# A forward transform over four token residues, and two placements around it

## The reference

```python
def hyena_filters(L, ...):
    ...                                   # a small network over positions gives h [L, order, 2, width]
    kern = concat([fwd, zeros(1), bwd[:0:-1]], axis=0)
    kern = kern / sum(abs(kern), axis=0)  # the filter norms
    return rfft(kern, axis=0)

def long_conv(u, k_f, skip):              # L = 512 tokens
    y = irfft(rfft(u, n=2 * L) * k_f, n=2 * L)[:L]
    return y + u * skip

z = parts[0]
for o in range(2):                        # two orders
    z = parts[o + 1] * long_conv(z, k_f[:, o], skip[o])
return (z * silu(gate)) @ w_out
```

## Time and profile before

| what | value |
| --- | --- |
| runs | 2197.36 us median of 3 (2193.96 to 2201.46) |
| profiled execution | 2202.59 us, span 2200.8 us |
| PE busy | 2095.3 us, 95% |
| PEld busy | 1611.6 us, 73% |
| DVE busy | 1372.0 us, 62% |
| ACT busy | 816.5 us, 37% |
| POOL busy | 797.9 us, 36% |

### The profile page before, as it was taken

The page is one execution under the profiler, slowest core; times in us unless marked ns, Lnnn a source line. Parts: engine busy times, 40 slices in busy tenths (PEclk is TensorE's granted clock), DMA queues, the critical chain, the costliest instruction groups (busy, mean ns, idle before and its releaser), DMA issues. The chain is left out here.

```text
span 2200.8 us, 28268 instructions
## 1 busy us (share of the span) xinstructions
PE 2095.3 (95%) x11070; PEld 1611.6 (73%) x11070; DVE 1372.0 (62%) x2351; ACT 816.5 (37%) x1185; POOL 797.9 (36%) x478
## 2 busy tenths in 40 slices
PE   7949999999999999999999999999999989999998
PEld 6847788888878877888888866556877536777776
DVE  8563399995555567488882133358775674477752
ACT  3414333333233377333332242345663332322222
POOL 6614455554545511344444411121002432311232
PEclk9979999999999999999999999998999979999999
DMA  5032344443434511244443322021002213222311
GB/s 187 2 44 86 102 138 144 140 130 114 128 117 129 128 40 25 86 144 144 144 134 90 96 101 79 29 58 41 1 21 78 91 63 141 80 77 78 114 58 67
DMA packets 57891, 201.84 MB, mean 92 GB/s; under 512 B 10521, under 2 KB 11721, under 8 KB 54207
## 3 DMA queue, kind: packets, MB, share of 16 engines
q1 hardware_dynamic: 40464, 156.92, 22.6%
q0 software_dynamic: 13568, 41.94, 6.2%
q10 hardware_dynamic: 3728, 1.18, 0.3%
HBM read 179.04 MB, written 10.49 MB: 86 GB/s over the span
## 5 line engine op out<-in xcount | busy, mean ns | idle before, releaser
L1666 POOL TENSOR_TENSOR w_lo<-raw,w_hi 128x1024 fp32r<-128x1024 f32 (+1 forms) x224 | 564.8, 2522 | 828.3 <-ACT w_hi L1222 828.1
L1222 ACT ACTIVATE w_hi<-raw 128x1024 fp32r<-128x1024 f32 (+1 forms) x224 | 233.8, 1045 | 847.5 <-PE psum L678 654.6
L671 PE MATMUL psum<-h_hi,w_hi 128*128 128x512 f32 x800 | 319.1, 399 | 1.5 <-ACT h_hi L1316 1.0
L672 PE MATMUL psum<-h_hi,w_lo 128*128 128x512 f32 x800 | 311.7, 390 | 0.0
L678 PE MATMUL psum<-h_lo,w_hi 128*128 128x512 f32 x800 | 198.0, 389 | 0.0
L671 PE MATMUL psum<-f_lo,w_hi 128*128 128x512 f32 x480 | 189.6, 395 | 2.3 <-POOL w_lo L1666 2.2
L672 PE MATMUL psum<-f_lo,w_lo 128*128 128x512 f32 x480 | 187.2, 390 | 0.0
L671 PEld LDWEIGHTS psum<-h_hi,w_hi 128*128 128x128 f32 x800 | 150.3, 188 | 38.5 <-ACT h_hi L1316 3.3
L672 PEld LDWEIGHTS psum<-h_hi,w_lo 128*128 128x128 f32 x800 | 150.3, 188 | 32.1 <-issue 2.2
L678 PEld LDWEIGHTS psum<-h_lo,w_hi 128*128 128x128 f32 x800 | 150.0, 188 | 31.3 <-issue 0.2
L1212 ACT ACTIVATE big<-psum 128x384 f32<-128x384 f32 (+6 forms) x182 | 90.0, 532 | 164.9 <-PE psum L973 47.6
(11 more groups left out here) (433 smaller groups left out, 4167.9 us busy)
## 6 DMA issues: line engine op xcount, KB each, us to landing
raw<-in_ffn_w_up SPq DMA_DIRECT2D x88, 512.0 KB, 3.6
raw<-in_ffn_w_down SPq DMA_DIRECT2D x32, 512.0 KB, 3.6
raw<-in_hy_in SPq DMA_DIRECT2D x32, 512.0 KB, 5.7
ffn_buf<-in_ada_w POOLq DMA_DIRECT2D x28, 512.0 KB, 5.0
sq<-in_ada_w POOLq DMA_DIRECT2D x20, 512.0 KB, 5.4
raw<-in_ssm_w_glu SPq DMA_DIRECT2D x16, 512.0 KB, 3.6
spec<-big SPq DMA_DIRECT2D x8, 1024.0 KB, 4.1
big<-spec SPq DMA_DIRECT2D x8, 1024.0 KB, 4.8
```

Source lines behind the costliest of these rows:

```text
L671: pe.matmul(o, hi[:, k, :], h_of(k), start=k == 0, stop=False)
L672: pe.matmul(o, lo[:, k, :], h_of(k), start=False, stop=False)
L1222: act.activation(w_parts(n)[0], raw[:, (n % 4) * HALF:(n % 4) * HALF + w], ACT.Copy).then_inc(S["w_hi"], 1)
L1666: pool.tensor_tensor(lo, raw[:, (n % 4) * HALF:(n % 4) * HALF + w], hi.bitcast(F32), ALU.subtract) \
```

## The change

The forward transform no longer folds even and odd tokens with 256 frequencies. It takes the four residues of the token number modulo 4 and 128 frequencies, cosine and sine, one matmul call each: eight calls per pass in two steps of four (`z_quarters`). The other frequencies follow from two levels of sums on VectorE: `z_first` (eight operations of 512 columns per pass, in two steps) into `YW`, and `z_fold` (one of 1024 and two of 512 for each u) into `CS`. The products follow the fold in the same tile. `YW` is now written by `z_first` too, so `z_first` of a pass waits for the inverse of the pass before. The four tables have new tiles. The frequencies of the second half stand in reverse order, in the filters' transform too. The new table (`QUARTERS`, 512 KB) is loaded by GpSimd's queue after the filters' transforms, over a part of the old table that is then no longer read.

Besides, the filter norm stands behind the transforms of its unit on TensorE and behind the fold on VectorE, `FSUM` has two buffers, seven `keep_clock` matmuls stand before the first cumulative sums of the attention, and in the gate tiles ScalarE makes `z_hi(t - 1)` before the activation of tile t.

```diff
-        TURN_AT = {8: (0, 0), 11: (0, 1), 15: (1, 0), 19: (1, 1)}
-        SPECTRUM_AT = {9: 0, 10: 1, 12: 2, 14: 3, 16: 4, 18: 5, 20: 6, 22: 7}
-        BACK_AT = {13: (0, 0), 17: (0, 1), 21: (1, 0), 24: (1, 1)}
-        SPEC_LOAD_AT = {t + 4: u + 1 for t, u in SPECTRUM_AT.items() if u < 7} | {9: 0}
+        TURN_AT = {5: (0, 0), 9: (0, 1), 15: (1, 0), 20: (1, 1)}
+        QUARTER_AT = {6: (0, 0), 7: (0, 1), 12: (1, 0), 13: (1, 1), 18: (2, 0), 19: (2, 1), 23: (3, 0), 24: (3, 1)}
+        PRODUCT_AT = {8: 0, 9: 1, 14: 2, 15: 3, 20: 4, 21: 5, 25: 6, 26: 7}
+        BACK_AT = {11: (0, 0), 17: (0, 1), 22: (1, 0), 27: (1, 1)}
+        QUARTER_OF = (((0, 0), (0, 2), (1, 1), (1, 3)), ((0, 1), (0, 3), (1, 0), (1, 2)))
+        SPEC_LOAD_AT = {t + 4: u + 1 for t, u in PRODUCT_AT.items() if u < 7} | {6: 0}
...
@@ TensorE, cumulate
                 if h == 0:
+                    keep_clock(7, 7)
                     pe.wait_ge(S["neg_ready"], 2)
...
@@ TensorE, filter stage
                 if u < 3:
                     filters(u + 1)
-                    filter_norm(u)
                 for f in range(2):
...
                         fills(i, key)
+                if u < 3:
+                    filter_norm(u)
...
@@ TensorE, hyena stage
+            def z_quarters(p_, part):
+
+                if p_ == 0 and part == 0:
+                    pe.wait_ge(S["quarters_in"], 16)
+                for i_, (a, r) in enumerate(QUARTER_OF[part]):
+                    key = ("sp", p_, part, i_)
                     o = take(pe, key)
+                    pe.wait_ge(*free(("zt", p_ // 2, p_ % 2, r)))
+                    fills(pe.matmul(o, QUARTERS[:, a, r, :], ZT[:, r, :], start=True, stop=True), key)
...
@@ ScalarE, gate tiles
-                    evac(("zg", t), SILU_G[t % 2], func=ACT.Silu)
                     if t:
                         z_hi(t - 1)
+                    evac(("zg", t), SILU_G[t % 2], func=ACT.Silu)
...
@@ GpSimd, filter stage
-                        if u:
-                            pool.wait_ge(*full(("nrm", u - 1)))
-                        i = pool.tensor_copy(FSUM, FAB[0])
+                        if u >= 2:
+                            pool.wait_ge(*full(("nrm", u - 2)))
+                        i = pool.tensor_copy(FSUM[u % 2], FAB[0])
...
+            pool.wait_ge(*full(("fs", 3, 1, 3)))
+            pool.dma_start(QUARTERS, A["quarters"].rearrange("p (a r n) -> p a r n", a=2, r=4)) \
+                .then_inc(S["quarters_in"], 16)
...
@@ VectorE
+                    if f and u < 3:
+                        filter_norm(u)
...
+            def z_first(p_, part):
+                ks = [("sp", p_, part, a) for a in range(4)]
+                own()
+                if p_ and not part:
+                    dve.wait_ge(*full(("y", (p_ - 1) // 2, 4 * ((p_ - 1) % 2) + 3)))
...
+                step(TT(YW[:, 0, part, :], c, oc, ALU.add))
+                frees(TT(YW[:, 1, 3 * part, :], c, oc, ALU.subtract), ks[0])
+                step(TT(YW[:, 0, 3 - part, :], s_, os_, ALU.add))
+                x, y = (os_, s_) if part else (s_, os_)
+                frees(TT(YW[:, 1, 1 + part, :], x, y, ALU.subtract), ks[2])
+            def z_fold(u):
...
+                half_, cs = YW[:, u % 2], CS.rearrange("p a (s n) -> p a s n", s=2)
+                step(TT(cs[:, :, 0, :], half_[:, 0::2, :], half_[:, 1::2, :], ALU.add))
+                step(TT(cs[:, 0, 1, :], half_[:, 0, :], half_[:, 1, :], ALU.subtract))
+                step(TT(cs[:, 1, 1, :], half_[:, 3, :], half_[:, 2, :], ALU.subtract))
+                own()
...
-                if n - 1 in SPECTRUM_AT:
-                    after = z_products(SPECTRUM_AT[n - 1])
                 if n in BACK_AT:
                     z_back(*BACK_AT[n])
-                if n - 1 in SPECTRUM_AT:
-                    z_sums(SPECTRUM_AT[n - 1], after)
-                if n in SPECTRUM_AT:
-                    z_fold(SPECTRUM_AT[n])
+                if n in PRODUCT_AT:
+                    u = PRODUCT_AT[n]
+                    z_fold(u)
+                    z_sums(u, z_products(u))
+                if n in QUARTER_AT:
+                    z_first(*QUARTER_AT[n])
```

More of the change, by code:

```diff
@@ L391, in build @@
         YW = bigv(12288, 4096).rearrange("p (f a n) -> p f a n", f=2, a=4)
+        QUARTERS = bigv(16384, 1024).rearrange("p (a r n) -> p a r n", a=2, r=4)
         DFT = bigv(16384, 4096)
@@ L409, in build @@
         FE = bigv(12288, 4096).rearrange("p (d s n) -> p d s n", d=2, s=4)
-        FSUM = sq[:, 0:512]
+        FSUM = [sq[:, 512 * i:512 * i + 512] for i in range(2)]
         FAB = [scr[:, 1024 + 512 * i:1536 + 512 * i] for i in range(2)]
@@ L1038, in filter_norm @@
                 for c in range(4):
-                    i = pe.matmul(o[:, c:c + 1], FSUM[:, c * P:(c + 1) * P], mat("ones")[:, 0:1], start=True, stop=True)
+                    i = pe.matmul(o[:, c:c + 1], FSUM[u % 2][:, c * P:(c + 1) * P], mat("ones")[:, 0:1], start=True, stop=True)
                 fills(i, key)
@@ L1077, in z_turn @@
                             pe.wait_ge(*((S["z_ready"], k + 1) if o_ else free(("z0", k))))
-                        p0 = t // 2 + 256 * (t % 2)
-                        i = pe.transpose(o[:, c * P:(c + 1) * P], Z0[:, k, p0:p0 + 255:2], mat("ident"))
+                        i = pe.transpose(o[:, c * P:(c + 1) * P], Z0[:, k, t:t + 509:4], mat("ident"))
                     fills(i, key)
[L1082 to L1085, removed]
-                    o = take(pe, key)
[L1087 to L1092, removed]
+            def z_quarters(p_, part):
[3 more added lines that the diff above has]
+                    key = ("sp", p_, part, i_)
+                    o = take(pe, key)
+                    pe.wait_ge(*free(("zt", p_ // 2, p_ % 2, r)))
+                    fills(pe.matmul(o, QUARTERS[:, a, r, :], ZT[:, r, :], start=True, stop=True), key)
             def z_back(o_, hf):
@@ L1120, in convolve @@
                     z_turn(*TURN_AT[t])
-                if t in SPECTRUM_AT:
-                    u = SPECTRUM_AT[t]
-                    z_spectrum(u // 4, (u // 2) % 2, u % 2)
+                if t in QUARTER_AT:
+                    z_quarters(*QUARTER_AT[t])
                 if t in BACK_AT:
@@ L1559, in z_turn, with z_odd @@
                 if 2 * o_ + hf:
-                    act.wait_ge(*full(("sp", 4 * o_ + 2 * hf - 1, 3)))
+                    act.wait_ge(*full(("sp", 2 * o_ + hf - 1, 1, 3)))
                 for t in range(4):
                     evac(("zt", o_, hf, t), ZT[:, t, :])
-            def z_odd(u):
-                if u:
-                    act.wait_ge(S["cs_ready"], 2 * u)
-                    act.wait_ge(*free(("sp", u - 1, 0)))
-                    act.wait_ge(*free(("sp", u - 1, 2)))
+            def z_odd(p_, part):
+                n = 2 * p_ + part - 1
+                if n >= 0:
+                    act.wait_ge(*free(("sp", n // 2, n % 2, 0)))
+                    act.wait_ge(*free(("sp", n // 2, n % 2, 2)))
                 for a, i in ((1, 0), (3, 1)):
-                    evac(("sp", u, a), OCS[:, i, :])
+                    evac(("sp", p_, part, a), OCS[:, i, :])
             def z_skip(o_, hf):
@@ L1594, in _ @@
                     if t == 1:
-                        act.wait_ge(*full(("sp", 7, 3)))
-                    evac(("zg", t), SILU_G[t % 2], func=ACT.Silu)
+                        act.wait_ge(*full(("sp", 3, 1, 3)))
                     if t:
                         z_hi(t - 1)
+                    evac(("zg", t), SILU_G[t % 2], func=ACT.Silu)
                 if n in TURN_AT:
                     z_turn(*TURN_AT[n])
-                if n in SPECTRUM_AT:
-                    z_odd(SPECTRUM_AT[n])
+                if n in QUARTER_AT:
+                    z_odd(*QUARTER_AT[n])
                 if n - 1 in TURN_AT:
@@ L1783, in _ @@
                     if q == 0:
-                        if u:
-                            pool.wait_ge(*full(("nrm", u - 1)))
-                        i = pool.tensor_copy(FSUM, FAB[0])
+                        if u >= 2:
+                            pool.wait_ge(*full(("nrm", u - 2)))
+                        i = pool.tensor_copy(FSUM[u % 2], FAB[0])
                     else:
                         pool.wait_ge(S["abs_used"], 8 * u + q)
-                        i = pool.tensor_tensor(FSUM, FSUM, FAB[q % 2], ALU.add)
+                        i = pool.tensor_tensor(FSUM[u % 2], FSUM[u % 2], FAB[q % 2], ALU.add)
                     i.then_inc(S["abs_used"], 1)
@@ L2442, in z_fold @@
                 dve.wait_ge(*free(ks[3]))
[L2443 to L2448, removed]
+                c, s_, oc, os_ = ps(ks[0]), ps(ks[2]), OCS[:, 0, :], OCS[:, 1, :]
+                step(TT(YW[:, 0, part, :], c, oc, ALU.add))
[4 more added lines that the diff above has]
+            def z_fold(u):
+                if u % 2 == 0:
+                    own()
+                    for part in range(2):
+                        for a in (0, 2):
```

(9 more changed lines are left out.)

12 lines of the change are left out of this document (3 added, 9 removed).

## The result

| kernel | median | runs | ratio to before (95%) |
| --- | --- | --- | --- |
| before | 2199.41 us | 4, 2193.96 to 2203.96 | |
| changed | 2219.1 us | 4, 2216.88 to 2221.7 | 1.0082 [1.0065, 1.0099] |

The change makes the kernel slower by 0.8%: 19.7 us between the medians, 22.3 predicted. The profiled execution took 2219.94 us, span 2218.1.

What follows compares the result with a forecast made beforehand. TensorE's own instructions were taken to bound the kernel; +26.8 us (hyena stage), -2.7 (filter stage) and -1.8 (keep_clock) gave +22.3, 2219.7 us against the 2197.36 median; range 2204 to 2232.

Steps and rivals of the forecast that it cites:

- The bound: Whole kernel: TensorE, busy 95% of the span, sets the time; other engines matter only where it waits for them.
- the order decides: Hyena stage: each pass's two products stand at consecutive tiles, serial on VectorE, and the inverse on TensorE waits for both.
- The stage, +26.8: Hyena stage: 61.5 us of new waits and lost clock, less 27.5 of TensorE work and 7.2 of old waits.
- The prediction's four sums: Hyena stage, per pass: time to the inverse's end with waits and slow clock; losses 12.4, 12.4, 17.1 and 19.6 us.
- The clock: Inverses on TensorE: idling before each second half drops the granted clock to 0.50, adding 3.1 us to each.
- both effects show every time that their cause is there: Hyena stage: argument that splits always stretch VectorE operations and waits always lower the clock, against a faster result (chance 0.09).
- The hits: Products on VectorE: additions of two SBUF tensors are stretched while GpSimd splits weights; eight, at 2.15 us each.
- The rule weighed in the prediction: Trainium skill: a VectorE instruction with two SBUF inputs and a GpSimd instruction reading SBUF contend; the second fully blocks.
- the constant: Products on VectorE: a fixed 2.15 us for each operation stretched by a GpSimd split.
- The bound of 2.4 us for a hit: Products on VectorE: a stretched operation costs what is left of the split, at most 2.4 us instead of 2.15.
- The filter stage, -2.7: Filter stage: norm behind the spectra gains 1.25 us, less 0.35 for VectorE's small operations, three times; bounds 0 and -4.6.
- keep_clock, -1.8: Attention: seven matmul calls fill TensorE's 3.51 us wait before the first cumulative sums; 1.8 us faster, 0 if the clock falls.

Runs made afterwards that it cites:

- Holding the clock: Changed kernel with keep_clock matmuls (14, 14, 6 and 8 calls) before the waits of the inverses' second halves: 2211.97 us; run again, 2215.21 us.
- the run without them: Changed kernel where GpSimd writes zeros as low parts of the weights of tiles 8 to 29 instead of subtracting: 2198.33 us, 0.9999 of before.
- the one with six tiles: Changed kernel reordered: five or six tiles from a pass's first quarter step to its inverse, products two apart in passes 1 to 3: 2193.79 us, 0.9973 of before.

## Why the prediction was right

**The bound and the order decides: held.** TensorE gives back 27.5 us (64 records of the forward transform, each step of four calls 3.43 us as before) and waits for two products in series at each inverse. No quarter step waits.

**The stage, +26.8 against +22.5.** The prediction's four sums run from the tile before a pass's products to the end of its inverse: 44.4, 44.4, 43.7 and 44.3 us. The timeline gives 43.9, 42.8, 43.4 and 42.4. That is 4.4 less, and the miss in the stage is 4.3. Two terms hold it:

- The second product was ready 34.2, 34.2, 33.2 and 33.5 us after that tile (34.4, 34.4, 33.7 and 34.3 predicted): 1.8 us, mostly from passes 3 and 4.
- The clock: the second halves take 37.4 us together, 9.8 above 4 x 6.9, where 4 x 3.1 = 12.4 was put: 2.6 us. The size of 3.1 came from one spell, and that one was among the longest of those seen (below). Holding the clock gave 8.2. The prediction argued that "both effects show every time that their cause is there"; for the clock this did not hold (last section).

The hits were 2.2 us each, as in the sum; that they carry as much as the whole slowdown is shown by the run without them, and that another order can carry them without loss by the one with six tiles. The rule weighed in the prediction (the Trainium skill, SBUF — State Buffer, "Who interferes with whom") agrees with the trace and fares about as well as the constant. All eight stretched operations started with 2.3 to 2.4 us of a split left and took 2.1 to 2.2 us more; the fold's L2466 started with 1.09 left and took 0.95 more. Seven of the eight splits last 2.8 to 3.4 us instead of 2.36, but only because each first waits for the operation that VectorE has under way: L2478 follows L2477 0.41 us after its split started, and that split lasts 2.77; L2497 follows L2494 0.91 us after, and that one lasts 3.26. So both things happen that the prediction set against each other: GpSimd waits for VectorE's running operation, and the next one waits for GpSimd. The bound of 2.4 us for a hit held.

**The filter stage, -2.7 against about -0.4: wrong.** The step "gain at most 1.87 each, half of it if the slow clock ends when it did" held for the norm itself (0.95). What the prediction left out is that the spells of low clock move with the work: the transforms of the last unit, which took 14.0 us in the old order, took 16.9 to 17.0 in four profiles of the new one (the changed kernel and the norm alone among them) and 15.7 in six. In the changed kernel the granted clock is 0.50 from 1820 to 1824, inside them; in the kernel before it is 1.00 all through them. Why the spell comes back there is open. From the first work of this stage to the end of the last transforms, profiles of the old order have 97.6, 96.7 and 95.9 us, those of the new one 97.1 and 95.5 in the changed kernel and 97.2 with the norm alone; all ten of the new order lie between 95.5 and 97.4, 96.2 in the mean, against 96.7. A gain of 0 to 2 us is not excluded; it is below what these profiles and times tell.

**keep_clock, -1.8: mechanism shown, size open.** From the first of these sums to TensorE's next piece of work it is 3.35 us (779.86 to 783.21) instead of 5.25 (782.23 to 787.48), so 1.9 us are gone there. The filter stage starts on average at 1740.4 in ten profiles with the edit (1738.1 to 1743.5) and at 1742.0 in three without (1741.1 to 1743.0): the right size, but the two ranges overlap.

**The sum.** +22.5 - 0.4 leaves 22.1 in the stages, and the whole profile shows +17.3, the medians +19.7 and +21.2. The 4.7 us by which this profile started its filter stage earlier than that of before are partly keep_clock and partly the scatter just shown; one profile cannot split them. That 22.3 came so near the medians is partly luck: the loss in the hyena stage was put 4.3 us too high and the gain in the filter stage 2.3 too high, so half of the one error hid behind the other.

## What to carry to other kernels

Count the work of an engine that is not the bottleneck between two points where the bottleneck waits for it, not its share of the span: VectorE was 62% busy, and moving its pieces next to each other cost more than 27.5 us of TensorE work saved. Price its operations with the neighbour that shares SBUF running, and see whether the pieces can stand two tiles apart: the same transform went from 0.8% slower to 0.3% faster by its tables and the order within a tile alone. An edit that removes low-clock time from one place has to be judged over the whole stage, since the next wait can bring it back elsewhere.

## What the runs showed of the hardware

The same wait did not always bring the same clock. Before the last inverse of the old order TensorE idled 2.73, 2.72 and 2.73 us in three kernels; the second half behind it took 10.18 us in the kernel before, and in the ones with keep_clock alone and the norm alone:

```profile
2086.80 7.17 PE L1106 MATMUL psum<-big 128*128 128x256 f32 x32 [2.72 <-DVEq L2489]
```

```profile
2090.96 8.79 PE L1106 MATMUL psum<-big 128*128 128x256 f32 x32 [2.73 <-DVEq L2490]
```

So one idle of this length costs 0 to 3 us, and waits of 3.3 to 9.5 us gave halves of 8.6 to 10.2: the length of the wait does not set the price either.

Contention took from both sides, in turn: a split of 2.36 us went to 2.77 and 3.26 by the 0.41 and 0.91 us that it waited for the VectorE operation under way, and the next VectorE operation waited for what was left of it (1.22 to 3.43 us). A GpSimd instruction that only writes (0.95 us) left the VectorE operations that started meanwhile at 1.22 and 0.68 us.
